# The grouped mixture of experts: one fixed tile of 128 slots for each expert, the down product of expert e-1 beside gate and up of expert e, and a loop for further tiles

## The reference, cut to what matters

```python
def grouped_moe(u, w_router, router_bias, w_gate, w_up, w_down):
    t = u.reshape(b * s, d)                                   # 640 x 1024
    scores = jax.nn.softmax((t @ w_router).astype(jnp.float32), axis=-1)
    ...                                                       # top-1 group, top-2 experts in it
    combine = jnp.sum(jax.nn.one_hot(eidx, N_EXPERTS, dtype=jnp.float32) * wsel[..., None], axis=1)
    hg = jnp.einsum('td,edf->tef', t, w_gate)                 # w_gate, w_up: 16 x 1024 x 256
    hu = jnp.einsum('td,edf->tef', t, w_up)
    h = jax.nn.silu(hg) * hu * combine.astype(t.dtype)[..., None]
    y = jnp.einsum('tef,efd->td', h, w_down)                  # w_down: 16 x 256 x 1024
    return y.reshape(b, s, d)
```

## Time and profile before

| | |
|---|---|
| median of 3 runs | 2197.0 us (2195.05 to 2199.16) |
| the profiled execution's own time | 2203.22 us |
| its span in the trace | 2201.6 us |
| PE busy / weight loads | 1639.7 us (74%) / 1383.9 us (63%) |
| DVE busy | 1380.1 us (63%) |
| ACT busy | 848.5 us (39%) |
| POOL busy | 526.1 us (24%) |
| DMA | 307.20 MB, mean 140 GB/s |

### The profile page before, as it was taken

The page is one execution under the profiler, slowest core; times in us unless marked ns, Lnnn a source line. Parts: engine busy times, 40 slices in busy tenths (PEclk is TensorE's granted clock), DMA queues, the critical chain, the costliest instruction groups (busy, mean ns, idle before and its releaser), DMA issues.

```text
span 2201.6 us, 29454 instructions
## 1 busy us (share of the span) xinstructions
PE 1639.7 (74%) x8840; PEld 1383.9 (63%) x8840; DVE 1380.1 (63%) x2062; ACT 848.5 (39%) x1294; POOL 526.1 (24%) x338
## 2 busy tenths in 40 slices
PE   3798688888897951888448968887899886458880
PEld 1578455578897751667337965555899875446660
DVE  1457577889845353667562947778987256447754
ACT  3112455661123031667322225656311322147651
POOL 4222000014423213223223310000343232122231
PEclk6799789999999955999859978999899998579995
DMA  8121144312222531988821203441123162169975
GB/s 313 51 73 58 45 154 138 122 30 58 73 63 77 210 134 53 317 313 310 309 77 58 69 33 121 148 154 49 39 60 85 39 230 105 67 223 318 341 256 210
DMA packets 192595, 307.20 MB, mean 140 GB/s; under 512 B 10793, under 2 KB 146089, under 8 KB 185185
## 3 DMA queue, kind: packets, MB, share of 16 engines
q1 hardware_dynamic: 165696, 218.12, 30.3%
q0 software_dynamic: 16176, 46.23, 5.9%
q10 hardware_dynamic: 10560, 40.90, 4.9%
HBM read 275.58 MB, written 39.59 MB: 143 GB/s over the span
## 4 chain that ended last, share of the span: by engine, by line
PE 42%; DVE 20%; issue 18%; DMA 7%; POOL 5%; ACT 5%; DVEq 1%; ACTq 0%; POOLq 0%; SPq 0%
PE ps L472 10%; PE ps L458 5%; PE ps L650 5%; PE ps L718 4%; POOL w_lo L1852 4%; PE ps L536 4%; DMA raw<-in_w_down 3%; PE ps L734 3%; PE ps L404 2%; DVE probs L1393 2%; PE ps L516 2%; PE ps L680 1%; PE ps L545 1%; PE ps L518 1%; DVE gu_lo L1222 1%
## 5 line engine op out<-in xcount | busy, mean ns | idle before, releaser
L1852 POOL TENSOR_TENSOR w_lo<-raw,w_hi 128x2048 fp32r<-128x2048 f32 (+1 forms) x68 | 299.8, 4414 | 736.8 <-ACT w_hi L879 702.9
L472 PE MATMUL ps<-u_hi,w_hi 128*128 128x320 f32 x768 | 245.7, 320 | 41.5 <-POOL w_lo L1852 30.0
L879 ACT ACTIVATE w_hi<-raw 128x2048 fp32r<-128x2048 f32 (+1 forms) x68 | 109.2, 1610 | 357.2 <-PE ps L458 154.4
L472 PE MATMUL ps<-u_lo,w_hi 128*128 128x320 f32 x768 | 243.7, 317 | 0.0
L472 PE MATMUL ps<-u_hi,w_lo 128*128 128x320 f32 x768 | 243.3, 317 | 0.0
L1504 DVE SCALAR_TENSOR_TENSOR cv<-glu,convw,cv 128x670 f32<-128x670 f32 x240 | 234.6, 1056 | 0.0
L472 PEld LDWEIGHTS ps<-u_hi,w_hi 128*128 128x128 f32 x768 | 150.0, 195 | 45.2 <-issue 33.3
L1409 DVE TENSOR_TENSOR pt_lo<-ps,pt_hi 128x512 fp32r<-128x512 f32 x160 | 108.6, 690 | 67.3 <-ACT pt_hi L986 65.4
L472 PEld LDWEIGHTS ps<-u_lo,w_hi 128*128 128x128 f32 x768 | 150.0, 195 | 0.1
L472 PEld LDWEIGHTS ps<-u_hi,w_lo 128*128 128x128 f32 x768 | 150.0, 195 | 0.0
L986 ACT ACTIVATE pt_hi<-ps 128x512 fp32r<-128x512 f32 x160 | 93.4, 597 | 135.7 <-PE ps L536 134.7
(11 more groups left out here) (319 smaller groups left out, 4138.6 us busy)
## 6 DMA issues: line engine op xcount, KB each, us to landing
raw<-in_w_ada SPq DMA_DIRECT2D x52, 1024.0 KB, 4.9
raw<-in_w_in SPq DMA_DIRECT2D x48, 512.0 KB, 4.9
raw_x<-in_w_gate SPq DMA_DIRECT2D x32, 512.0 KB, 5.2
raw_x<-in_w_up SPq DMA_DIRECT2D x32, 512.0 KB, 6.4
raw<-in_w_down SPq DMA_DIRECT2D x16, 1024.0 KB, 8.5
raw<-in_w_gate SPq DMA_DIRECT2D x32, 512.0 KB, 4.4
raw<-in_w_up SPq DMA_DIRECT2D x32, 512.0 KB, 5.7
raw_x<-in_w_down SPq DMA_DIRECT2D x16, 1024.0 KB, 8.4
```

What stands on the lines that cost most here:

```text
L472: ins = mm(ps[:, b, 0:HALF], (w_hi, w_lo)[w][:, s, cols(k):cols(k) + P], xs[x][:, k, half * HALF:(half + 1) * HALF], start=(k == 0 and w + ...
L879: act(w_hi[:, n % 2, 0:k], raw[:, n % 2, 0:k], ACT.Copy).then_inc(*A.up("a_hi", "w_hi", n))
L1852: g_.tensor_tensor(w_lo[:, n % 2, 0:k], raw[:, n % 2, 0:k], w_hi[:, n % 2, 0:k].bitcast(F32), ALU.subtract).then_inc(*G.up("g_lo", "w_lo", n))
```

## The change: what it does

- The 16 experts get one fixed tile of 128 slots each (slots 128e to 128e+127), so the loop over experts needs no registers: it is written out with constant waits. Pairs beyond 128 of an expert go to up to 9 further tiles (`OVT`), which a hardware loop handles after the experts. That loop runs at least once, and as often as there are such tiles (once in each layer on these inputs). It loads the three matrices of its expert again.
- On PE the down product of expert e-1 stands behind gate and up of e and the transposes of e+1. The copy out of PSUM moves from ACT to DVE.
- `xe` and `ye` are doubled, and two gathers stand ahead. Gathers take their indices from `tab` directly. An empty slot is skipped in the gather too, so `xe` is zeroed once in a layer by a POOL memset of 2048 columns.
- A unit of the experts is now one whole matrix (gate, up or down), with 8 KB in a row for each partition, row 8p+c of the matrix in partition p. To match this, the transposes read every eighth column of `xe` (`k:D:KC`) and every second of `hx`. Units come in the order of `GATE_UP_DOWN`: gate and up of e+2 ahead of down of e+1.
- POOL makes the lo parts of the first five units (all of expert 0, gate and up of expert 1) ahead of the scatter of the tables, and the down parts of all experts in the loop; DVE makes gate and up of the experts from 2 on.
- The two rank matmuls become 20 smaller ones, which sum over the token tiles in PSUM, and the DVE chain behind them has fewer steps; parts that don't depend on the router are written earlier.

```diff
@@ PE, the experts
+            for t in range(NT):
+                for i in range(t):
+                    mm(ps[:, b, t * NE:(t + 1) * NE], ones[:, :], cnt[:, i, :], start=(i == 0), stop=False)
+                mm(ps[:, b, t * NE:(t + 1) * NE], tri[:, :], cnt[:, t, :], start=(t == 0), stop=True)
+            for t in range(NT):
+                ins = mm(ps[:, b, 256:256 + NE], ones[:, :], cnt[:, t, :], start=(t == 0), stop=(t == NT - 1))
...
+            xe_transposes(0)
+            for e in range(NE):
+                eng.wait_ge(*T.at("xt_split", e))
+                eng.wait_ge(*T.at("w_lo", UNIT_OF[e, 0]))
+                eng.wait_ge(*T.at("w_lo", UNIT_OF[e, 1]))
+                gate_up((e + 1) % 2).then_inc(*T.up("gu_full", "gu_full", e))
+                if e + 1 < NE:
+                    xe_transposes(e + 1)
+                if e:
+                    down_of(e - 1)
+                eng.wait_ge(*T.at("h_ready", e))
+                h_transposes().then_inc(*T.up("ht_full", "ht_full", e))
+            down_of(NE - 1)
+
             eng.wait_ge(*T.at("starts"))
+            eng.wait_ge(*T.at("y_drained", NE - 1))
...
+            with eng.Fori(0, n_over) as j:
+                o = o0 + j + 1
+                eng.wait_ge(sems("ov_landed"), 16 * o)
                 for k in range(KC):
-                    ins = nc.tensor.transpose(ps[:, k // 4, (k % 4) * P:(k % 4 + 1) * P], xe[:, k * P:(k + 1) * P], ident[:, :])
+                    ins = nc.tensor.transpose(ps[:, k // 4, (k % 4) * P:(k % 4 + 1) * P], xe[:, 0, k:D:KC], ident[:, :])
+                ins.then_inc(sems("ov_xt"), 1)
+                eng.wait_ge(sems("ov_split"), o)
+                eng.wait_ge(sems("ov_gu_lo"), 2 * o + 2)
+                gate_up(1).then_inc(sems("ov_gu"), 1)
...
@@ SP, the loads
-                               io[w][l, e, kh * 512:(kh + 1) * 512, :].rearrange("(c p) n -> p c n", p=P))
-                              for i, w in enumerate(("w_gate", "w_up"))))
...
+            for e, k in GATE_UP_DOWN:
+                n = UNIT_OF[e, k]
+                load(n, (r(n, (KC, KC, 2)[k]), io[("w_gate", "w_up", "w_down")[k]][l, e, :, :].rearrange("(p c) n -> p c n", p=P)))
...
@@ ACT
-            hi_expert(U_MOE + 2)
+            hi_expert(UNIT_OF[0, 2])
             eng.wait_ge(*A.at("u2_out"))
+            hi_expert(UNIT_OF[1, 0])
+            hi_expert(UNIT_OF[1, 1])
...
             for e in range(NE):
+                eng.wait_ge(*A.at("gu_full", e))
+                act(sg[:, :], ps[:, 2, 0:DE], ACT.Silu).then_inc(*A.up("sg_ready", "sg_ready", e))
+                if e + 1 < NE:
+                    xt_hi_of(e + 1)
+                if e + 2 < NE:
+                    hi_expert(UNIT_OF[e + 2, 0])
+                eng.wait_ge(*A.at("ht_full", e))
+                act(ht_hi[:, :, :].rearrange("p c n -> p (c n)"), ps[:, 3, 0:2 * P], ACT.Copy).then_inc(*A.up("ht_hi", "ht_hi", e))
+                if e + 2 < NE:
+                    hi_expert(UNIT_OF[e + 2, 1])
+                if e + 1 < NE:
+                    if e:
+                        eng.wait_ge(*A.at("y_full", e - 1))
+                    hi_expert(UNIT_OF[e + 1, 2])
...
+            with eng.Fori(0, n_over) as j:
+                o = o0 + j + 1
+                eng.wait_ge(sems("ov_raw0"), 16 * o)
+                act(expert_part(1, 0, 1), over_raw(0, 2), ACT.Copy).then_inc(sems("ov_hi"), 1)
+                eng.wait_ge(sems("ov_xt"), o)
+                act(xt_hi[:, :, :].rearrange("p (a c) n -> p a (c n)", a=2), ps[:, 0:2, :], ACT.Copy).then_inc(sems("ov_xthi"), 1)
+                eng.wait_ge(sems("ov_raw1"), 16 * o)
+                act(expert_part(1, 1, 1), over_raw(1, 3), ACT.Copy).then_inc(sems("ov_hi"), 1)
...
@@ DVE
+            for e in range(NE):
+                eng.wait_ge(*V.at("gu_full", e))
+                eng.wait_ge(*V.at("sg_ready", e))
+                v.scalar_tensor_tensor(out=hx[:, :], in0=ps[:, 2, DE:2 * DE], scalar=tab[:, e, 2:3].bitcast(F32), in1=sg[:, :],
+                                       op0=ALU.mult, op1=ALU.mult).then_inc(*V.up("h_ready", "h_ready", e))
+                if e + 1 < NE:
+                    xt_lo_of(e + 1)
+                if e:
+                    y_of(e - 1)
+                eng.wait_ge(*V.at("ht_hi", e))
+                split_ht().then_inc(*V.up("ht_split", "ht_split", e))
+                if e + 2 < NE:
+                    lo(UNIT_OF[e + 2, 0])
+                    lo(UNIT_OF[e + 2, 1])
...
@@ POOL
-            for n in range(U_MOE, U_MOE + 2):
+            for n in range(U_MOE, U_MOE + 5):
                 lo(n)
...
+            g_.memset(xe[:, :, :], 0.0).then_inc(*G.up("g_c", "xe_zero"))
...
+            for e in range(3):
+                gather_of(e)
             for e in range(NE):
+                if e + 3 < NE:
+                    gather_of(e + 3)
+                if e:
+                    scatter_of(e - 1)
+                if e + 1 < NE:
+                    lo(UNIT_OF[e + 1, 2])
...
+                scatter(0, sidx[:, :]).then_inc(sems("ov_sent"), 16)
+            scatter_of(NE - 1)
```

More of the change, by code:

```diff
@@ L693, in _, with xe_transposes, gate_up @@
                 eng.wait_ge(*T.at("drained", last[b]))
+            def xe_transposes(e):
+                eng.wait_ge(*T.at("xe_landed", e))
+                for k in range(KC):
+                    ins = nc.tensor.transpose(ps[:, k // 4, (k % 4) * P:(k % 4 + 1) * P], xe[:, e % 2, k:D:KC], ident[:, :])
+                ins.then_inc(*T.up("xt_full", "xt_full", e))
+            def gate_up(i):
+                for k in range(KC):
+                    for w, x in MM3:
+                        ins = mm(ps[:, 2, :], (xt_hi, xt_lo)[x][:, k, :], (gu_hi, gu_lo)[w][i][:, k, :],
+                                 start=(k == 0 and w + x == 0), stop=(k == 7 and w == 1))
+                return ins
@@ new lines, in h_transposes, with down @@
+            def h_transposes():
+                for c in range(2):
+                    ins = nc.tensor.transpose(ps[:, 3, c * P:(c + 1) * P], hx[:, c:DE:2], ident[:, :])
+                return ins
+            def down(i):
+                for half in range(2):
+                    for c in range(2):
+                        for w, x in MM3:
+                            ins = mm(ps[:, 4 + half, :], (ht_hi, ht_lo)[x][:, c, :], (dn_hi, dn_lo)[w][i][:, c, half * 512:(half + 1) * 512],
+                                     start=(c == 0 and w + x == 0), stop=(c == 1 and w == 1))
+                return ins
@@ new lines, in _, with split_xt @@
+            eng.wait_ge(*V.at("v", V.steps))
+            v.tensor_scalar(start[:, 0:OVT], start[:, 0:OVT], float(NE - 1), None, ALU.min).then_inc(*V.step())
+            v.tensor_tensor(tbase[:, :], tbase[:, :], start[:, OVT:OVT + 1], ALU.add).then_inc(*V.step())
+            eng.wait_ge(*V.at("v", V.steps))
+            v.tensor_copy(start_i[:, :], start[:, :]).then_inc(*V.up("v_start", "starts"))
+            def split_xt():
+                return v.tensor_tensor(xt_lo[:, :, :].rearrange("p (a c) n -> p a (c n)", a=2), ps[:, 0:2, :],
+                                       xt_hi[:, :, :].rearrange("p (a c) n -> p a (c n)", a=2).bitcast(F32), ALU.subtract)
@@ L1791, in _ @@
         g_.memset(tri[:, :], 1.0).then_inc(*G.up("g_c", "tri0"))
-        g_.memset(ye[:, :], 0.0).then_inc(*G.up("g_c"))
         eng.wait_ge(*G.at("tri0"))
@@ new lines, in scatter, with gather_of @@
+            def scatter(of, index):
+                return eng.indirect_dma_start(out=y_d, out_offset=bass.IndirectOffsetOnAxis(ap=index, axis=0),
+                                              in_=ye[:, of, :], in_offset=None,
+                                              bounds_check=2 * NTOK - 1, oob_is_err=False)
+            def gather_of(e):
+                if e >= 2:
+                    eng.wait_ge(*G.at("xt_full", e - 2))
+                    eng.sem_inc(sems("passed_G"), 1)
+                gather(e % 2, tab[:, e, 0:1]).then_inc(*G.up(f"xe_landed{e % 2}", "xe_landed", e, by=16))
```

402 lines of the change are left out of this document (196 added, 206 removed).

## The result

The changed kernel takes **2219.5 us** (median of 4 runs, 2215.9 to 2221.3), the kernel before 2197.1: ratio **1.0106, 95% interval 1.0087 to 1.0125**, 22 us slower. The prediction was 2191.5, with a range up to 2214: wrong in sign, and outside its range. The profiled execution took 2221.3 us with a span of 2219.8, against 2203.2 and 2201.6.

What follows compares the result with a forecast made beforehand. PE's chain was taken to bound the experts, with late tiles waiting for weights. A layer summed as 9.0 - 0.5 + 8.9 + 14 x 10.2 + 37.1 = 197.3 us against 200.0, giving 2191.5 us, range 2170 to 2214.

Steps and rivals of the forecast that it cites:

- The rank matmuls: Routing: 18 more at 0.21 us, 3.8 us, 1.2 of it beside DVE work; counted nothing net, bounds 2 either way.
- The shorter DVE chain: Routing, behind the rank matmuls: some 14 steps fewer at 0.18 us each, 2.5 us saved.
- The lock: Routing: three POOL lo parts block DVE over the shared SBUF port, 9.0 us a layer, bounds 0 to 13.5.
- The start: Between routing and first gather: the xe memset replaces a lo part and index copy, 0.5 us earlier a layer.
- The tiles: Experts: 8.9 us to the second gate and up, then 14 periods of 10.2, including 0.4 for strided reads.
- weights late: Expert loop: larger pieces bring no DMA rate, period 11.0 us, in all 2214 us; chance 0.15.
- point of decision: Expert period of 10.4 us, from which weights arriving late make a layer reach the old 200.0 us.
- The further tile: Behind expert 15: a chain of 25.6 us to the end of its gate and up, 37.1 with the tail.
- The tail behind it: After the further tile's gate and up: 10.2 us as before, plus 1.3 for the scatter of expert 15.
- Strided loads: Transposes in the experts: strided weight loads take twice as long, period 10.7 us, in all 2206; chance 0.12.
- no lock: Routing: DVE keeps the port or POOL's parts miss its two-input instructions, 9 us less a layer, 2174; chance 0.23 with bare period.
- costly tail: Further tile costs 41 us, giving back the gain: +1.2 us a layer, in all 2199; chance 0.10.

Runs made afterwards that it cites:

- experiment 1: Changed kernel with only POOL's order altered, its three lo parts moved out of DVE's routing chain to behind the tab load and first gathers: 2198.2 us, ratio 0.9992.
- experiment 3: Changed kernel with 6 rank matmuls in place of 20, the totals summed on DVE: 2207.4 us, ratio 1.0032.
- experiment 8: Changed kernel loading only half of each w_down in the loop of 16 experts, same instructions, wrong numbers: 2209.1 us, ratio 1.0041.
- experiment 2: Kernel before, with POOL's third lo part (down of expert 0) moved from behind the tab load to ahead of the wait for the ranks: 2206.7 us, ratio 1.0023.
- Experiment 10: Changed kernel with POOL's lo parts moved, 6 rank matmuls, up's parts earlier in the further tile, and the xe memset ahead of the rank wait: 2177.5 us, ratio 0.9913.
- experiment 6: Changed kernel with the order of before within a tile on PE, ACT and DVE, down of e behind its own transposes: 2249.2 us, ratio 1.0225.
- experiment 7: Changed kernel with the old row layout, pieces of 1 KB (4 KB for down) and transposes without a stride: 2238.0 us, ratio 1.017.

## Why the prediction was wrong

Mean of both layers, predicted -2.7 a layer, measured +10.7. The 13.4 between them, by the prediction's own steps:

- **The rank matmuls, "I count nothing net, and 2 us either way": this step failed.** Measured +4.5 us (22.9 in experiment 1, with no lock, against 18.4). The row of the router's matmuls says x32, and I read 32 calls at 0.21 us. They are 16 calls of two instructions each, as one call with x2 now shows, so a call costs 0.43. Eighteen more are 7.7 us and not 3.8; measured 8.7 - 1.1 = 7.6. Of that 1.2 should have lain beside DVE's work on the weights of the pairs; only 0.4 did, since that work had hidden the two calls of before already, and 7.2 came onto the path (8.9 - 1.7). The shorter DVE chain gave back 2.6, as said. A call and an instruction could have been told apart with the trace of before, where the source has 5 token tiles of KC = 8 calls in each of two layers, 80 calls, and the line has 160 instructions:

```profile
L680 PE MATMUL ps<-wr,u_t x160: 234/374/374, 801.1 to 1894.4; 128*128 128x16 f32 x160
```

- **The lock, 9.0: right mechanism, size 11.0.** All three parts got in. The second and third cost 4.3 and 2.3, forecast 4.2 and 2.5. The first I had begin half a us later than it did, behind the last of the `pair` instructions, so that DVE could run on to 1900.06; it began 0.07 us ahead of one of them and blocked it whole, 4.3 us for 2.3. That the third caught only half an instruction, as forecast, was luck: in layer 1 of experiment 3 and in experiment 8 it took a whole one, 13.1 in all, near the upper bound of 13.5.
- **The start, -0.5: between -0.1 and +1.4 to the first gather.** I set the memset against the lo part and the index copies that stood there. But the landing of `tab` had covered the lo part, and taking it away in the kernel before won 0.3 us at most (experiment 2), while the memset stands behind the landing with its whole 1.8 + 0.9, about what the way over the index copies had cost. The rest of the +1.4 is the later load of `tab` in layer 2, which stays open. Experiment 10 got 2.5 back at the first gather. From there to the first hx 0.4 to 0.9 were won.
- **The tiles, 8.9 + 14 x 10.2 = 151.7: 157.5 and 154.7.** PE's order brought what was forecast (experiment 6). The 5.8 and 3.0 too many are mostly weights (experiment 8 takes 6.9 and 4.5 away): I took the 417 GB/s of w_ada's rows as they were, the measured rate is 375, between that and the 348 of the rival *weights late*. That 10.2 came so near was luck in part. Its 0.4 for the strided reads was nothing (0.89 us for eight transposes, as before), and in its place stand the waits for weights, which the forecast had at nothing; without the stride it would have been 9.8. In the form of the sum the periods are (157.5 - 8.9) / 14 = 10.6 and 10.4, for 10.2: between the forecast and that rival, and at or past its point of decision.
- **The further tile, 25.6 to the end of its gate and up: 25.8 and 26.3.** Right. The tail behind it was forecast as before's and 1.3 for the scatter of expert 15; it is 2.9 and 2.5 longer, 1.4 a layer more. (In layer 1 the same stretch is 17.3 to 18.7 us in all later kernels with this loop, for 20.2 here, so some of it belongs to this one execution.)

In sum, mean of the layers: 4.5 + 2.0 + 1.1 - 0.6 + 4.4 + 0.4 + 1.4 = 13.2 of 13.4. *Strided loads* fell (experiment 7: a load takes 188 ns where the transposes follow each other at 0.11 us, so it hides, against my "128 of a load and 128 of a matmul, without slack"), *no lock* fell (1 and 2), *costly tail* fell in the part it named. Nearly every term came out dearer than forecast, none by much against 2200 us. In measured numbers the tiles gave 22.5 us a layer, the further tile took 15.0 of it and the tail 2.7; the 4.8 that were left stood against 15.6 in the routing. The range held each rival alone, but no case had two together, and here the rank product lay outside its bounds of 2 while the lock, the start and the period all lay on the dear side of their values.

## What to carry to other kernels

Before a row's count is multiplied, compare it with a loop in the source whose length is known: a call can stand as more than one instruction. A serial chain of short DVE instructions is the worst place for a long POOL instruction that reads SBUF; one such part can cost its whole length, however small the DVE instruction (4.3 of 4.5 us here, or 2.3 where it was caught halfway), so it belongs behind the chain or beside DVE work that has an input in PSUM (the split `xt_lo` took its usual 1.23 us beside a lo part). When the work ahead of a wait is taken out, the wait stays: look for what that work had covered. Where a blocked instruction is caught is chance, so a lock is better given as a range. And where a sum of many small terms ends near zero, the cases should hold two of its errors together.
